# Dealing the steps of a recurrence anew in a kernel of four mixer layers, with loads and returns moved ahead of two stage borders

## The reference, cut to what matters

```
z = hn @ w_in;  q, k, v, g ...                       # layer 1
o_b = stick_breaking(q, k, v);  mixed = concat(o_a * silu(ga), o_b * silu(gb));  h += mixed @ w_out
# layer 2, one step for every token, state is 64x64 for each of 16 heads
decay = exp(-exp(w_log));  a = sigmoid(a0 + (xa @ a1) @ a2);  kk = k*k_k / norm(k*k_k);  k = k*(1 + (a-1)*k_a)
state = state*w - (state @ kk)[..., None]*(kk*a) + v[..., None]*k;   y = state @ r
y = head_norm(y)*gain + bias + bonus;   h += (y * silu(g)) @ w_out
h += sigmoid(h @ gate) * (p @ proj)                  # end of every layer
```

## Time and profile before

| | us |
|---|---|
| median of 3 runs (lowest, highest) | 3959.63 (3945.48, 3961.38) |
| the profiled execution, its time | 3956.88 |
| its span | 3954.9 |
| PE busy | 3651.2 (92%) |
| DVE busy | 2020.1 (51%) |
| ACT busy | 1663.2 (42%) |
| mean granted TensorE clock | 0.944 |

### The profile page before, as it was taken

One profiled execution on the slowest core, in us unless ns is written; L12 is line 12 of the kernel. 1 busy time (PEld: TensorE's weight loads), 2 busy tenths in 40 slices (PEclk: granted clock), 3 DMA queues, 4 the chain that ended last, 5 costly groups with the idle time before them and its releaser, 6 DMA issues. The chain is left out here.

```text
span 3954.9 us, 48229 instructions
## 1 busy us (share of the span) xinstructions
PE 3651.2 (92%) x18866; PEld 2973.8 (75%) x18866; DVE 2020.1 (51%) x3934; ACT 1663.2 (42%) x3109; POOL 107.4 (3%) x119
## 2 busy tenths in 40 slices
PE   7999789999997999999898999999879999999799
PEld 6888548768875777777676877777768788888686
DVE  3144342453345777775335455555555456666542
ACT  3222461454442444333225444444443466665420
POOL 0011220000000000000000000000000000000000
PEclk9999899999997888888899999999979999999799
DMA  4333402112222212120411101010032121110311
GB/s 142 115 133 104 141 27 102 54 67 106 97 74 84 56 43 54 52 57 25 173 38 62 28 28 33 28 28 28 33 112 75 49 65 38 43 38 17 131 67 43
DMA packets 219706, 265.61 MB, mean 67 GB/s; under 512 B 62685, under 2 KB 142677, under 8 KB 218457
## 3 DMA queue, kind: packets, MB, share of 16 engines
q1 hardware_dynamic: 219480, 262.53, 20.2%
HBM read 191.95 MB, written 70.52 MB: 66 GB/s over the span
## 5 line engine op out<-in xcount | busy, mean ns | idle before, releaser
L328 PE MATMUL bank<-wh,XH 128*128 128x512 f32 x1344 | 552.6, 411 | 39.1 <-DVE wl L312 19.6
L328 PE MATMUL bank<-wl,XH 128*128 128x512 f32 x1344 | 528.0, 393 | 0.0
L328 PE MATMUL bank<-wh,XL 128*128 128x512 f32 x1344 | 527.9, 393 | 0.0
L2519 PE MATMUL bank<-XH,wh 128*128 128x512 f32 x1040 | 425.8, 409 | 26.7 <-DVE wl L2508 25.1
L2519 PE MATMUL bank<-XH,wl 128*128 128x512 f32 x1040 | 410.7, 395 | 0.0
L2519 PE MATMUL bank<-XL,wh 128*128 128x512 f32 x1040 | 409.4, 394 | 0.0
L328 PEld LDWEIGHTS bank<-wh,XH 128*128 128x128 f32 x1344 | 255.4, 190 | 102.0 <-issue 38.0
L328 PEld LDWEIGHTS bank<-wh,XL 128*128 128x128 f32 x1344 | 255.6, 190 | 60.2 <-issue 10.0
L328 PEld LDWEIGHTS bank<-wl,XH 128*128 128x128 f32 x1344 | 254.9, 190 | 55.2
L328 PE MATMUL bank<-XH,wh 128*128 128x512 f32 x704 | 280.3, 398 | 7.9 <-DVE XL L1549 7.9
L312 DVE TENSOR_TENSOR wl<-raw,wh 128x1024 fp32r<-128x1024 f32 x128 | 157.6, 1244 | 251.3 <-ACT wh L303 249.9
(11 more groups left out here) (406 smaller groups left out, 7056.9 us busy)
## 6 DMA issues: line engine op xcount, KB each, us to landing
sc_zt<-stage SPq DMA_DIRECT2D x88, 256.0 KB, 2.0
raw<-in_att_w_in SPq DMA_DIRECT2D x33, 512.0 KB, 4.2
raw<-in_even_w_in SPq DMA_DIRECT2D x32, 512.0 KB, 5.3
raw<-in_odd_w_in SPq DMA_DIRECT2D x32, 512.0 KB, 4.3
raw<-in_rec_w_in SPq DMA_DIRECT2D x32, 512.0 KB, 4.0
sc_h<-H SPq DMA_DIRECT2D x24, 512.0 KB, 2.6
sc_z<-stage SPq DMA_DIRECT2D x40, 256.0 KB, 2.0
z<-sc_z SPq DMA_DIRECT2D x8, 1024.0 KB, 5.8
```

Source lines behind the costliest of these rows:

```text
L328: done = e.matmul(out, lhsT, rhs, start=k == 0 and j == 0, stop=k == NK - 1 and j == 2)
L2519: done = e.matmul(bank[:, :], x[:, k, :], y[:, k, ts], start=k == 0 and j == 0, stop=k == NK - 1 and j == 2)
```

## The change

1. `Stick`'s tables and the loads of heads 0 to 2 (`sp_first`) are issued by SP inside EvenIn's list, ahead of the store of tile 62. Head 3 stays behind EvenIn's last store and no longer waits for heads 0 to 2's place in the old order. PE, DVE, ACT and POOL enter Stick on `freed`, which has no DMA in it, in place of `ends`.
2. In `PLACED`, `('tail', 1, 5)` and `('bonus')` go from slot 5 to slot 6 (ahead of the solve), `('gates')` from 6 to 7, `('lora', 0)` from slot 8 to the end of slot 14, and ACT's part of `scan` becomes an entry `keys` in slot 10.
3. During block 7, rows 0 to 6 of the mixed result are loaded back into `kk` and `tm` in turns (`fetch`), and split into `XH` and `XL` (`back`), which now lie on tiles that the last block has finished with; layer end 1's first four weight tiles are split too (`weights`). `LAST` says in which slots. Row 7 is never stored: its halves are split straight from `zo` (`end`). The weights of layer end 1 use semaphores of their own. The order of the allocations is changed so that the tiles cover each other.
4. PE makes 7 of the 8 parts of layer end 1's first tile (`pe_first`) before the last transposes of the recurrence, and the last part once row 7 is there. PE no longer waits for `Rwkv.ends` as a whole, which are now `xlow(7, 1)` alone, the low part of row 7's second half.

```diff
 # EvenIn.sp, inside the loop over tiles n
                 if n == 60:
                     following.first(e)
+                if n == 62:
+                    self.guest.sp_first(e)
 # Stick
+    def sp_first(self, e):
         wait_all(e, self.even_in.ret.read)
         wait_all(e, [(self.even_in.sent[u % 4], (u,)) for u in range(52, 56)])
         (the three tables)
+        for h in range(3):
+            self.sp_head(e, h)
+    def sp(self, e, before):
+        e.wait_ge(*self.even_in.ret.gated.at(NS - 1))
+        self.sp_head(e, 3)
         wait_all(e, before)
 # PLACED
-    5: ((-1, 'tail', 1, 4), (-1, 'tail', 1, 5), (1, 'pack', 1), (1, 'bonus'), (2, 'load')),
-    6: ((1, 'solve', 4), (0, 'gates')),
-    7: ((1, 'solve', 2),),
-    8: ((2, 'lora', 0), (1, 'solve', 3)),
+    5: ((-1, 'tail', 1, 4), (1, 'pack', 1), (2, 'load')),
+    6: ((-1, 'tail', 1, 5), (1, 'bonus'), (1, 'solve', 4)),
+    7: ((1, 'solve', 2), (0, 'gates')),
+    8: ((1, 'solve', 3),),
-    10: ((1, 'solve', 2),),
+    10: ((2, 'keys'), (1, 'solve', 2)),
-    14: ((2, 'norm'), (0, 'tail', 0, 2), (1, 'solve', 3)),
+    14: ((2, 'norm'), (0, 'tail', 0, 2), (1, 'solve', 3), (2, 'lora', 0)),
+LAST = {2: (("fetch", 0),), 5: (("fetch", 1),), 8: (("back", 0), ("fetch", 2), ("weights", 0)), 11: (("back", 1), ("fetch", 6), ("weights", 1)),
+        14: (("back", 2), ("fetch", 4), ("weights", 2)), 17: (("back", 6), ("fetch", 5), ("weights", 3)),
+        20: (("back", 4), ("fetch", 3), ("back", 5)), 23: (("back", 3),)}
+FETCHED = (0, 1, 2, 6, 4, 5, 3)
 # end of rwkv_order
-    order += [("tail", 7, 1, part) for part in range(6)]
+            if p == 7:
+                order.extend((x[0], 7, *x[1:]) for x in LAST.get(3 * n + j, ()))
+    order += [("tail", 7, 1, 0), ("end", 7, 0), *[("tail", 7, 1, part) for part in range(1, 6)], ("end", 7, 1)]
 # Rwkv.sp_part: a fetch waits until the row before last in its buffer has been split
+        if what == "fetch":
+            k = rest[0]
+            at = FETCHED.index(k)
+            if at >= 2:
+                e.wait_ge(*self.xlow.at(FETCHED[at - 2], 1))
...
+            e.dma_start(self.row_back(k), self.zt[k * P:(k + 1) * P, :]).then_inc(*self.fetched[at % 2].up(k))
 # Rwkv.pe_part, tail part 5
+            if (p, half) == (7, 1):
+                self.then.pe_first(e)
 # Rwkv.ac_part and ve_part
+        if what == "back":
+            e.wait_ge(*self.fetched[FETCHED.index(k) % 2].at(k))
+            wait_all(e, self.row_free(k))
+            e.activation(c.XH[:, k, :], self.row_back(k), ACT.Copy).then_inc(*self.xhigh.up(k, 1))
...
+            e.tensor_tensor(self.c.XL[:, k, :], self.row_back(k), f32(self.c.XH[:, k, :]), ALU.subtract).then_inc(*self.xlow.up(k, 1))
```

More of the change, by code:

```diff
@@ L667, in ac @@
         wait_all(e, before)
[L668 to L672, removed]
+        if self.mixed is None:
+            self.w.ac(e, 0)
         self.w.ac(e, 1)
@@ L739, in ve @@
         wait_all(e, before)
[L740 to L744, removed]
+        if self.mixed is None:
+            self.w.ve(e, 0)
         self.w.ve(e, 1)
@@ L1726, in rwkv_order @@
     some(0, "bonus", "gates")
-    some(1, "scan")
+    some(1, "scan", "keys")
     some(0, ("tokens", 0), ("scores", 0))
@@ L1819, in __init__ @@
         self.zeros, self.eye, self.cleared = (c.flag("po") for _ in range(3))
-        self.ends = [(self.out, (7, 1)), *[(f, ()) for f in self.stored]]
+        self.fetched, self.xhigh, self.xlow, self.following = c.each("dma", 2), c.flag("ac"), c.flag("ve"), None
+        self.then = None
+        self.ends = [(self.xlow, (7, 1))]
     def beside(self, e, t, part):
@@ L1887, in sp @@
                 following.first(e)
+            elif what == "weights" and rest[0] == 0:
+                following.sp(e, 0)
     def sp_part(self, e, what, p, *rest):
-        if what == "tables":
+        if what == "fetch":
[3 more added lines that the diff above has]
+                e.wait_ge(*self.xlow.at(FETCHED[at - 2], 1))
+            elif at == 0:
+                e.wait_ge(*self.fact.at("al", 7))
+            else:
+                e.wait_ge(*self.side.at("bonus", 7, 1))
+            for half in range(2):
+                e.wait_ge(*self.stored[half].at(k))
+            e.dma_start(self.row_back(k), self.zt[k * P:(k + 1) * P, :]).then_inc(*self.fetched[at % 2].up(k))
+        elif what == "tables":
             for t, n in ((self.cols2, "cols2"), (self.after, "after"), (self.upto, "upto"), (self.heads2, "heads2")):
@@ L1920, in sp_part @@
             self.sp_unpack(e, p)
-        elif what == "tail" and rest[1] == 5:
+        elif what == "tail" and rest[1] == 5 and p < 7:
             half = rest[0]
@@ L2146, in ac_part @@
         c = self.c
-        if what == "begin":
+        if what == "back":
+            k = rest[0]
+            e.wait_ge(*self.fetched[FETCHED.index(k) % 2].at(k))
+            wait_all(e, self.row_free(k))
+            e.activation(c.XH[:, k, :], self.row_back(k), ACT.Copy).then_inc(*self.xhigh.up(k, 1))
+        elif what == "end":
+            half = rest[0]
+            e.wait_ge(*self.out.at(7, half))
+            e.wait_ge(*self.step.at("u", 7, NS - 1))
+            e.activation(c.XH[:, 7, HALVES[half]], self.zo[half][:, :], ACT.Copy).then_inc(*self.xhigh.up(7, half))
+        elif what == "weights":
+            if rest[0] == 0:
+                for name in ("be", "ka", "rkr"):
+                    e.wait_ge(*self.fact.at(name, 7))
+                e.wait_ge(*self.lor.at(7, 1, 1))
+            self.following.ac_part(e, 0, rest[0])
+        elif what == "begin":
             wait_all(e, self.shifted())
@@ L2187, in ac_prepare @@
                     .then_inc(*self.sig.up(p, j, h))
-        elif what == "scan":
+        elif what == "keys":
             e.wait_ge(*self.kin.at(p))
@@ L3562, in vector @@
             even_in.ve(e, [])
-            stick.ve(e, even_in.ends)
+            stick.ve(e, even_in.freed)
             end0.ve(e, stick.ends, odd_in)
@@ L3586, in gpsimd @@
             even_in.po(e, [])
-            stick.po(e, even_in.ends)
+            stick.po(e, even_in.freed)
             odd_in.po(e, end0.ends)
```

96 lines of the change are left out of this document (58 added, 38 removed).

## The result

The changed kernel takes **3987.44 us** (median of 5 runs, 3960.53 to 3994.55); the kernel before, run beside it, takes 3954.61 (median of 5). The ratio is **1.0061, 95% interval 1.0034 to 1.0088**: slower by 0.6%. Forecast was 3934, range 3908 to 3956. The profiled execution took 3987.44 (span 3985.6, granted clock 0.932) against 3956.88 (3954.9, 0.944).

What follows compares the result with a forecast made beforehand. DVE was taken to bound slots 6 to 14, PE slots 15 to 18 and block 7, head arrival the Stick border. Terms -9.7 - 19.2 + 12.0 + 3.0 - 11.1 = -25.0 us gave 3931.9, median-adjusted and called 3934; range 3908 to 3956.

Steps and rivals of the forecast that it cites:

- Part C: Recurrence, blocks 0 to 5: first gate product moved from slot 8 to 14, +12.0 us, and 12 more table loads, +3.0.
- Part B: Slots 5 and 6: pn loaded ahead of the store of zo, solve 3.4 us earlier, -19.2 us over 7 blocks.
- Part A: Border of EvenIn and Stick: tables and heads 0 to 2 issued earlier, head 3 arriving at 433.6, -9.7 us.
- What is late next is PE with the scores for the mask; they come about 1 us before they are wanted: Slots 5 and 6: after the earlier pn load, PE's scores come next, about 1 us early, supporting -19.2 us.
- My third rival: Slots 5 and 6: Part B gives nothing, pn sharing DMA with key loads and PE's scores late; 3953 us, chance 0.13.
- The sign that I had named: Wrong if block times stay at 80 us or more without the pn wait; then PE, not DVE, bounds slots 6 to 14.
- so I take 2.0: Slot 14: product at half clock, 3.78 less PE's 1.74 us wait for the state, 2.0 a block, +12.0 us.
- The other falls into ACT's idle time of slot 16: Slot 16: the second extra table load a block, 1.28 us on ACT, is hidden and adds nothing.
- rival 4: Table switches on the path: slot 16's load unhidden, lw late by 0.96; 10.4 us over six blocks, 3944, chance 0.10.
- Its removal from slot 8 frees 1.98 us of PE and 2.5 of ACT where DVE is the bound, worth nothing: Slot 8: taking the gate product out frees PE and ACT time while DVE is the bound, 0 us.
- rival 2: Clock falls before slot 11, scan stalls 5.6 us in five blocks, slot 14's products cost 3.8; 3970 us, chance 0.07.
- Part D: Block 7 and behind: rows returned and split during block 7, tile 1 starts earlier, -11.1 us, bounds 5 and 20.

Runs made afterwards that it cites:

- e1: The changed kernel with the first gate product put back from slot 14 to slot 8: 3949 us, ratio 0.9976 to the kernel before.
- e16: The kernel before with the early head loads alone: 3944 us, ratio 0.9975.
- e4: The kernel before with only slots 5 to 7 in the new order (pn loaded ahead of the store of zo): 3957 us, ratio 1.0004.
- e2: The changed kernel with slots 5 to 7 as in the kernel before: 3997 us, ratio 1.0099 to the kernel before.
- e13: The changed kernel, gate product ahead of slot 14's norm, plus a one-column sigmoid behind the norm's root: 3968 us, ratio 1.0026 to the kernel before.
- e15: The kernel before with a one-column sigmoid at the end of slot 14 (two more table loads a block): 3979 us, ratio 1.0045.
- e9: The changed kernel with the first gate product still in slot 14 but ahead of the norm: 3951 us, ratio 0.9988 to the kernel before.
- e3: The kernel before with only the first gate product moved from slot 8 to slot 14: 4006 us, ratio 1.0118.
- e7: The kernel before with the first gate product made once more at the end of slot 14, into an unread bank: 3970 us, ratio 1.0025.
- e8: The kernel before with early heads, new slots 5 to 7 and keys in slot 10 (no gate move, no returned rows): 3961 us, ratio 0.9995.
- e5: The changed kernel with the first gate product in slot 12 in place of 14: 3925 us, ratio 0.9918 to the kernel before.
- e11: The changed kernel with the first gate product in slot 12 and slots 5 to 7 as before: 3984 us, ratio 1.0047 to the kernel before.
- e14: The changed kernel with the gate product first in slot 13: 3960 us, ratio 0.9985 to the kernel before.
- e6: The changed kernel with the first gate product made once more in slot 8, into an unread bank: 3975 us, ratio 1.0044 to the kernel before.
- e10: The kernel before with only the first gate product moved from slot 8 to slot 12: 3980 us, ratio 1.0058.

## Why the prediction was wrong

The forecast was -25 us, the measured change +33 by the two medians and +24 by the ratio. e1, which takes back only the gate product's move, splits the miss of 49: that move costs 34 us here where +15 was forecast, and all the rest together gains 9.5 where 40 was forecast. The step that failed worst is therefore in Part C, and Part B's gain hung on an assumption about slot 8.

**Part A was right**: -9.7 forecast, -9.9 measured (e16); head 3 scaled at 433.02 for 433.6.

**Part B failed in the step "What is late next is PE with the scores for the mask; they come about 1 us before they are wanted".** The mechanism (the solve 3.4 us earlier) was there, and slots 3 to 5 are 30.1 us shorter in each kernel of the slot table that has it. But the step looked one operation ahead only. Where the product stays in slot 8 (e4), what was late next was that product, on the path by 1.8 us a block ("a PE product in slot 8 isn't" paid held only for the late solve), and then the scan behind the product of slot 11 at the low clock: `lw` +22.6 us against `pn` -20.3. In the changed kernel neither is late, and the edit is worth some 15 us (e2, intervals that meet). My third rival had the size, no change, with another reason. The sign that I had named came too: blocks 0 to 3 and 5 take 85 us and more though the wait for `pn` is gone.

**Part C failed.** In the changed kernel three things show. First, "so I take 2.0" for the product in slot 14. The text had named the case where "the norm's product already fills the gap" (3.8) and not taken it. It was the case in five of six blocks: the norm ran at the 1.2 GHz level, the product behind it took 3.77 us, and slots 12 to 14 are 33.2 us longer. Second, "The other falls into ACT's idle time of slot 16". ACT had idle time, but the work behind the load had a consumer three hops on. Twelve loads cost 15 us (e13) and 18 (e15) for the +3.0 of the sum; that is rival 4, with more than its price. Third, block 7: the sum put a lower clock there at nothing, and its first seven intervals are 14.3 us longer. The order inside the slot accounts for 29 us (e9), of which the table loads are about 15 (e13). The other 14 fit block 7, which runs at 1.00 in e9 and e13 and at 0.74 in the changed kernel; that is one profiled execution of each.

A fourth step, "Its removal from slot 8 frees 1.98 us of PE and 2.5 of ACT where DVE is the bound, worth nothing", fails in the kernel before, where the move alone costs 47 us (e3). With the product left in slot 8 and made again in slot 14 the price is 10 us (e7), with the table loads alone 18 (e15); these two make 28, and if they simply add, the other 19 or so are what slot 8's removal does. It shows as a wait of 24.5 us at the scan, with the gate product of slot 11 at the low clock in four of six blocks. That is rival 2's mechanism, which I had at 0.07 because five of six blocks showed the fall in slot 14 or later. In the changed kernel it did not occur: the scan waits 4.8 us in all, slots 9 to 11 are 6.5 us shorter than before, and of rival 2 only the second half came, the product at 3.8 us behind a late norm. What takes its place is the fall ahead of slot 14.

The Trainium skill (ScalarE: Activation LUTs, What ACT_TABLE_LOAD costs) has 2.66 us for a switch, of which 1.38 are a drain; 12 such switches would be 32 us of ACT time, an estimate from that page. The same page (Table sets: the hidden batching unit) wants calls batched by set. The rows show 1.28 for each of 36 loads and no drain, and 12 switches cost 15 to 18 us of the kernel's time (e13, e15), 1.3 to 1.5 each. So the advice to batch holds and the row's price was the better one, but the kernel paid it in full, which I had denied. Which of a block's two loads is paid isn't shown: in e15 the waits at `T` and at the scan grew by 9.0 us together, half of the 18.

**Part D**: -11.1 forecast, -7.5 measured with an uncertainty as large (e1 against e8). In e1's trace tile 1 starts 18.2 us behind the last y, 16.4 earlier than before (15.4 by the forecast's places), the last tail starts 4.6 us behind the last y (forecast 5.1) and seven of block 7's intervals cost 2.2 us more than in e8 (forecast 1.2). In the changed kernel's own trace block 7 runs at the low clock and its seven intervals take 57.9 us, 13.0 more than in e1. The returns alone don't do this: seven kernels with them (e1, e5, e9, e11 to e14) run block 7 at 1.00. The three that have both the returns and the gate product behind the norm (the changed one, e2 and e6) run it at 0.74, 0.93 and 0.78; why wasn't separated. How much of the 16.4 us the stages behind keep isn't shown either. (The working of the last fetch adds up to 1878.9, not 1879.2, which changes nothing.)

**The sum of single edits** (D by e1 against e8) is -9.9 + 1.6 + 46.7 - 7.5 = 31 us, for 24 measured. That the two are close is luck: the 46.7 and the 1.6 come with waits of 24.5 and 28.9 us at the scan that the changed kernel doesn't have, and its own loss lies elsewhere. With the product in slot 12 the same edits give -32 us: the parts don't add where one decides which engine is late and on which product the clock's fall lands. `keys` in slot 10 was never run alone, so what it adds is not known.

What stays open: what decides whether the clock falls ahead of slot 11, ahead of slot 14 or later, and so why slot 12 and not 10 keeps it up until the norm. Both fill PE; only the traces tell them apart, and I had no run that changed the clock without changing the order.

## What to carry to other kernels

Where two engines take turns, price the removal of work as carefully as its addition: a product in slot 8 that looked free beside a busy DVE could be moved away only at a price of 23 us, even to a slot with room (e10); yet with the solve early it was itself in the way, and slot 12 was the better place by 23 us (e5 against e1). Look in the trace for the product on which the clock's fall lands, before and after. When a wait is removed, walk the order to the next two or three waits of every engine, not to the first. Give a function that needs another table a place beside one that has it, and follow what the next root holds up through its stores and loads.

## What the runs showed of the hardware

A removed stall can cost exactly what it saves: in e4, 20.3 us less at `pn`, 22.6 more at `lw`, 0.0% in time. With 1.98 us less work on PE in slot 8, the product of slot 11 took 3.78 us in place of 1.98 in four of six blocks, one before (e3); but with that work left in place and the solve started earlier it did so in five (e4). The same six matmul groups in the same slot cost 10 us in one kernel (e7) and, with table loads and another place emptied, 47 in another (e3). And a sigmoid of 128 numbers a block cost 0.4% of the kernel, with the two table loads that it brings (e13, e15).
